# Second block's input kept on chip from the feed-forward stage, and one score matrix per tile in the gated recurrence

## The reference, cut to what matters

```python
for l in range(DEPTH):                       # first block, DEPTH = 1
    z = rmsnorm(h, mix_norm_g[l]); p = z @ w_in[l]
    y_a = s5_mixer(...)
    y_b = hgrn2_mixer(q, f, v, gate, lower_bounds[l], hgrn_norm_g[l])
    merged = sigmoid(gate_a) * (y_a @ w_ssm_proj[l]) + sigmoid(gate_b) * (y_b @ w_hgrn_proj[l])
    h = h + merged @ w_out[l]
    z = rmsnorm(h, ffn_norm_g[l])
    u = causal_dwconv(z @ w_up[l], conv_w[l], conv_b[l])
    h = h + (silu(u[..., :D_FF]) * u[..., D_FF:]) @ w_down[l]
x = rmsnorm(h[:, N_META:], final_norm_g)     # the second block's input
h = rms_norm(x, norm_mix_g[l])               # second block
projections = h @ w_in[l]                    # attention, rwkv7 and gates start from these
```

## Time and profile before

| what | value |
|---|---|
| median of the runs | 2699.37 us |
| the profiled execution's own time | 2700.83 us |
| its span, first to last instruction | 2699.0 us |
| mean granted TensorE clock | 0.969 of 2.4 GHz |
| hgrn2 | about 344 to 557 us |
| down projection of the feed-forward stage | 1009 to 1131.5 us |
| front | 1134.7 to 1357 us |
| experts (from their first weight load to the end) | 1734 to 2699 us |

### The profile page before, as it was taken

One profiled execution on the slowest core, in us unless ns is written; L12 is line 12 of the kernel. 1 busy time (PEld: TensorE's weight loads), 2 busy tenths in 40 slices (PEclk: granted clock), 3 DMA queues, 4 the chain that ended last, 5 costly groups with the idle time before them and its releaser, 6 DMA issues. The chain is left out here.

```text
span 2699.0 us, 45154 instructions
## 1 busy us (share of the span) xinstructions
PE 2467.9 (91%) x19448; PEld 1729.3 (64%) x19448; DVE 1188.4 (44%) x1949; ACT 736.2 (27%) x1175; POOL 126.7 (5%) x133
## 2 busy tenths in 40 slices
PE   8999878989999999899989988799989989899888
PEld 7998667789999998677777857543333333333232
DVE  7765756644556663266645576411111111111113
ACT  4221264433333432153423264310000000000001
POOL 1000022100000000002300030100000000000000
PEclk9999899999999999999999999999999999999999
DMA  5444441345322223333422235499999999999997
GB/s 165 138 131 117 95 183 60 112 158 191 126 97 87 93 84 128 131 114 130 135 83 90 66 117 201 185 403 431 431 431 430 430 431 430 431 431 430 430 431 290
DMA packets 156902, 612.36 MB, mean 227 GB/s; under 512 B 50400, under 2 KB 72032, under 8 KB 131680
## 3 DMA queue, kind: packets, MB, share of 16 engines
q1 hardware_dynamic: 127792, 574.59, 54.4%
q10 hardware_dynamic: 28912, 34.88, 4.0%
HBM read 568.02 MB, written 39.04 MB: 225 GB/s over the span
## 5 line engine op out<-in xcount | busy, mean ns | idle before, releaser
L3878 PE MATMUL moe_bank<-moe_ring,xg 128*64 128x512 f32 x2048 | 489.0, 621 | 89.7 <-DMA moe_ring<-in_w_exp_up 88.8
L3878 PEld LDWEIGHTS moe_bank<-moe_ring,xg 128*64 128x64 f32 x2048 | 154.2, 141 | 367.2 <-issue 358.0
L4168 DVE TENSOR_TENSOR moe_sg<-moe_sg,moe_bank 64x512 f32<-64x512 f32 x64 | 44.1, 690 | 576.9 <-ACT moe_sg L4036 576.9
L3908 PE MATMUL moe_bank<-moe_ring,moe_act_t 128*64 128x512 f32 x1008 | 227.0, 592 | 0.0
L68 PE MATMUL ffn_prod<-ffn_x_low,ffn_w_high 128*128 128x258 f32 x704 | 200.1, 284 | 5.8 <-PEq L138 5.8
L69 PE MATMUL ffn_prod<-ffn_x_high,ffn_w_low 128*128 128x258 f32 x704 | 200.1, 284 | 0.0
L68 PE MATMUL in_bank<-x_low,in_w_high 128*128 128x264 f32 x640 | 185.8, 290 | 15.3 <-DVE in_w_low L987 9.1
L70 PE MATMUL ffn_prod<-ffn_x_high,ffn_w_high 128*128 128x258 f32 x704 | 199.3, 283 | 0.0
L70 PE MATMUL in_bank<-x_high,in_w_high 128*128 128x264 f32 x640 | 183.5, 287 | 0.0
L69 PE MATMUL in_bank<-x_high,in_w_low 128*128 128x264 f32 x640 | 183.2, 286 | 0.0
L3908 PEld LDWEIGHTS moe_bank<-moe_ring,moe_act_t 128*64 128x64 f32 x1008 | 72.2, 137 | 143.5 <-issue 143.4
(11 more groups left out here) (586 smaller groups left out, 5062.9 us busy)
## 6 DMA issues: line engine op xcount, KB each, us to landing
moe_ring<-in_w_exp_gate SPq DMA_DIRECT2D x64, 2048.0 KB, 27.6
moe_ring<-in_w_exp_up SPq DMA_DIRECT2D x64, 2048.0 KB, 21.3
moe_ring<-in_w_exp_down SPq DMA_DIRECT2D x63, 2048.0 KB, 25.8
rw_w<-in_w_in SPq DMA_DIRECT2D x50, 512.0 KB, 3.3
ffn_w<-in_w_up SPq DMA_DIRECT2D x44, 512.0 KB, 4.1
in_w<-in_w_in SPq DMA_DIRECT2D x40, 512.0 KB, 3.8
ffn_w<-in_w_down SPq DMA_DIRECT2D x16, 704.0 KB, 4.1
p<-in_out ACTq DMA_DIRECT2D x32, 264.0 KB, 4.0
```

Of the source, the lines that this page charges most:

```text
L3878: last = nc.tensor.matmul(bank[64 * g:64 * g + 64, s], xe[:, (e // BATCH) % 2, k, at:at + CAPACITY], ring[:, slot_of(n, g), k * HALF:(k + ...
L3908: last = nc.tensor.matmul(bank[64 * h:64 * h + 64, 3 + e % 2], act_t[:, s, j], weights[:, at:at + HALF], start=(c == 0 and j == 0), stop=( ...
L4168: nc.vector.tensor_tensor(sg[0:CAPACITY, s], sg[0:CAPACITY, s], bank[64:64 + CAPACITY, s], ALU.mult).then_inc(act_ready, 1)
```

## The change: what it does, and the diff

(1) The feed-forward stage writes its result h into SBUF (`front_h`) and not to HBM. While it runs, ACT makes the next stage's x_high of each row tile but the last, and DVE the x_low. The gains are loaded and multiplied there. At its end SP loads the first two weight tiles of the front into slots that are free by then; ACT and DVE split them. The residual is loaded into `gate` and not into `u`. The front starts at once with tiles 0 and 1, and waits only for row tile 7. (2) In hgrn2, k_in has two copies, one with only the odd chunks and one with only the even ones filled (zero elsewhere); the scores are two matmuls that accumulate into one 128 x 128 matrix, one mask and one product follow. `QK_PARTS = 4` takes the place of the 3 in the counts.

```diff
 # conv_gated_ffn
         def res_of(m):
-            return u[:, m % 2, 1, 0:TO]
-        def out_of(m):
-            return y[:, m % 2, 0, 0:TO]
+            return gate[:, m % 2, 0:TO]
 # its SP
+                sp.dma_start(gains[:], gains_dram).then_inc(gains_loaded, 16)
                 for n in range(2, items):
...
                             if m < 2:
-                                sp.wait_ge(hidden_ready, FT - 1 + m)
+                                sp.wait_ge(hidden_ready, FT)
...
+                sp.wait_ge(w_ready, items - 2)
+                for n in range(2):
+                    sp.dma_start(first_w[:, n].rearrange("p k m -> p (k m)"), next_w_dram[n * P:(n + 1) * P, :]).then_inc(first_loaded, 16)
 # its ACT, in for m in range(kt), behind the two split_w_high
                     if m >= 1:
+                        act.wait_ge(gains_ready, 2)
                         act.wait_ge(out_ready, m)
-                        act.dma_start(out_dram[(m - 1) * P:m * P, :], out_of(m - 1)).then_inc(stored[(m - 1) % 2], 16)
-                act.wait_ge(out_ready, kt)
-                act.dma_start(out_dram[(kt - 1) * P:kt * P, :], out_of(kt - 1)).then_inc(stored[(kt - 1) % 2], 16)
-                for s in range(2):
-                    act.wait_ge(stored[s], 16 * kt // 2)
+                        nc.scalar.activation(next_high[:, m - 1], h[:, m - 1], ACT.Copy, scale=gain_both[:, m - 1:m]).then_inc(
+                            next_high_ready, 1)
+                act.wait_ge(first_loaded, 32)
+                act.wait_ge(prod_ready, items - 1)
+                for n in range(2):
+                    nc.scalar.copy(first_high[:, n], first_w[:, n]).then_inc(first_high_ready, 1)
 # its DVE, in for m in range(kt), behind the two split_w_low
-                    if m >= 2:
-                        dve.wait_ge(stored[m % 2], 16 * (m // 2))
-                    nc.vector.tensor_tensor(out_of(m), prod[:, m % 2, 0, 0, 0:TO], res_of(m), ALU.add).then_inc(out_ready, 1)
+                    nc.vector.tensor_tensor(h[:, m], prod[:, m % 2, 0, 0, 0:TO], res_of(m), ALU.add).then_inc(out_ready, 1)
+                    if m < kt - 1:
+                        dve.wait_ge(next_high_ready, m + 1)
+                        nc.vector.scalar_tensor_tensor(next_low[:, m], h[:, m], gain_both[:, m:m + 1], next_high[:, m].bitcast(F32),
+                                                       ALU.mult, ALU.subtract).then_inc(next_low_ready, 1)
+                    if m == kt - 2:
+                        for n in range(2):
+                            dve.wait_ge(first_high_ready, n + 1)
+                            nc.vector.tensor_tensor(first_low[:, n], first_w[:, n], first_high[:, n].bitcast(F32),
+                                                    ALU.subtract).then_inc(first_low_ready, 1)
 # hgrn2: POOL, DVE, PE
-                    nc.gpsimd.tensor_tensor(k_in[:, s], f(h), e_down[:, s], ALU.mult).then_inc(qk_ready, 1)
+                    for a in range(2):
+                        of = slice(1 - a, None, 2)
+                        nc.gpsimd.tensor_tensor(by_chunk(k_in[:, s, a])[:, of], by_chunk(f(h))[:, of], by_chunk(e_down[:, s])[:, of],
+                                                ALU.mult).then_inc(qk_ready, 1)
...
+                nc.gpsimd.memset(k_in[:], 0.0).then_inc(k_in_cleared, 1)
...
-                    nc.vector.tensor_tensor(scores[0:m, n % 2, :, 0:m], bank[0:m, 2, 0:2 * m].rearrange("p (a t) -> p a t", a=2),
-                                            mask[0:m, :, 0:m], ALU.mult).then_inc(scores_ready, 1)
+                    nc.vector.tensor_tensor(scores[0:m, n % 2, 0:m], bank[0:m, 2, 0:m], mask[0:m, 0:m], ALU.mult).then_inc(
+                        scores_ready, 1)
...
-                    nc.tensor.matmul(bank[0:m, 2, 0:2 * m], k_in[:, h % 2, span(i)], qq[:, h % 2, :, span(i)],
-                                     start=True, stop=True).then_inc(scores_made, 1)
+                    for a in range(2):
+                        last = nc.tensor.matmul(bank[0:m, 2, 0:m], k_in[:, h % 2, a, span(i)], qq[:, h % 2, a, span(i)],
+                                                start=(a == 0), stop=(a == 1))
+                    last.then_inc(scores_made, 1)
...
-                    for a in range(2):
-                        last = nc.tensor.matmul(bank[0:m, 3, 0:P], scores[0:m, n % 2, a, 0:m], turned[0:m, n % 3, 1],
-                                                start=(a == 0), stop=False)
+                    nc.tensor.matmul(bank[0:m, 3, 0:P], scores[0:m, n % 2, 0:m], turned[0:m, n % 3, 1], start=True, stop=False)
 # front
-                for k_tile in range(KT):
-                    act.dma_start(h[:, k_tile], hv[:, k_tile]).then_inc(h_loaded[k_tile], 16)
-                act.wait_ge(gains_ready, 2)
-                split_x_high(0)
-                split_w_high(0)
-                for k_tile in range(1, KT):
-                    split_x_high(k_tile)
-                split_w_high(1)
+                split_x_high(KT - 1)
...
-                for k_tile in range(KT):
-                    if k_tile == 1:
-                        split_w_low(0)
-                    split_x_low(k_tile)
-                split_w_low(1)
+                split_x_low(KT - 1)
...
-                        if n == 0:
-                            pe.wait_ge(x_low_ready, k + 1)
+                        if n == 0 and k == KT - 1:
+                            pe.wait_ge(x_low_ready, 1)
```

More of the change, by code:

```diff
@@ L360, in conv_gated_ffn @@
         out_ready = sem("out_ready")
-        stored = [sem(f"stored{s}") for s in range(2)]
+        gains_loaded = sem("gains_loaded")
+        gains_ready = sem("gains_ready")
+        next_high_ready = sem("next_high_ready")
+        next_low_ready = sem("next_low_ready")
+        first_loaded = sem("first_loaded")
+        first_high_ready = sem("first_high_ready")
+        first_low_ready = sem("first_low_ready")
         def piece_of(a, s):
@@ L1301, in hgrn2 @@
         ident = sb("ident", [P, P])
-        mask = sb("mask", [P, 2, P])
+        mask = sb("mask", [P, P])
         turned = sb("turned", [P, 3, 2, P])
-        scores = sb("scores", [P, 2, 2, P])
+        scores = sb("scores", [P, 2, P])
         states = sb("states", [P, RING, P])
@@ L2185, in tri_by_matrix, with front @@
     return tri_places(tri_dram, n).rearrange("(m r) t -> m (r t)", r=RCHUNK)
-def front(nc, stage, h_dram, gains_dram, w_dram, par_dram, mu_l_dram, lora_dram, ident_dram, x_high, x_low, scale, ident, raw, raw_l, out,
+def front(nc, stage, h, gains, gain_both, gain_squared, first_high, first_low, w_dram, par_dram, mu_l_dram, lora_dram, ident_dram, x_high, x_low, scale, ident, raw, raw_l, out,
           ar, bh, kh, v, bonus, ends, lat_g, x_dram, p_dram, w, w_high, w_low, masks_dram, tri_dram, lowers, flats, sweep):
@@ L2369, in products @@
                     s = n % 2
-                    pe.wait_ge(w_ready, n + 1)
+                    high, low = (first_high, first_low) if n < 2 else (w_high, w_low)
+                    if n >= 2:
+                        pe.wait_ge(w_ready, n - 1)
                     if n >= 4:
@@ L4251, in two_blocks @@
     h1 = scratch("h1", D_MODEL, KEPT)
-    h2 = scratch("h2", D_MODEL, SEQ)
+    early = ExitStack()
+    gains, gain_both, gain_squared = (early.enter_context(nc.sbuf_tensor(f"front_{name}", [P, n, KT], F32)) for name, n in (
+        ("gains", 2), ("gain_both", 1), ("gain_squared", 1)))
+    gain_both, gain_squared = gain_both[:, 0], gain_squared[:, 0]
+    x_place = -(-nc.sbuf_base // 32) * 32
+    next_high, next_low = (nc.alloc_sbuf_tensor_at(f"front_x_{part}", [P, KT, SEQ], F32R, offset=x_place + 4 * KT * SEQ * i)
+                           for i, part in enumerate(("high", "low")))
     with ExitStack() as keep:
@@ L4314, in two_blocks @@
                           merge_res, merge_e, x_raw, x_high, x_low, gain, d["ffn_norm_g"], sq_sum, w, w_high, w_low, first_weights)
-        conv_gated_ffn(nc, "ffn", h1, x_high, x_low, sq_sum, w, w_high, w_low, d["w_up"], d["conv_w"], d["conv_b"], d["w_down"], h2)
+        slot_bytes = 4 * 2 * D_MODEL
+        first_w, first_high, first_low = (
+            nc.alloc_sbuf_tensor_at(f"front_first_w{part}", [P, 2, KT, P], dt, offset=place + slot_bytes * at)
+            for part, dt, at in (("", F32, -2), ("_high", F32R, 0), ("_low", F32R, 2)))
+        h = conv_gated_ffn(nc, "ffn", h1, x_high, x_low, sq_sum, w, w_high, w_low, d["w_up"], d["conv_w"], d["conv_b"], d["w_down"],
+                           next_high, next_low, gains, gain_both, gain_squared, d["gains_2"], d["w_in_2"], first_w, first_high, first_low)
     x = scratch("x", D_MODEL, SEQ)
@@ L4326, in two_blocks @@
     with late, ExitStack() as keep:
+        x_high, x_low = next_high, next_low
+        keep.enter_context(nc.sbuf_tensor("front_x_room", [P, 2 * KT * SEQ + (x_place - nc.sbuf_base) // 4], F32))
         bonus = keep.enter_context(nc.sbuf_tensor("rw_bonus", [P, RW_X, SEQ], F32))
```

(1 more changed line is left out.)

78 lines of the change are left out of this document (35 added, 43 removed).

## The result

| | before | after |
|---|---|---|
| median of 4 runs each, us | 2697.89 (2694.58 to 2702.75) | 2725.58 (2724.41 to 2730.20) |
| profiled execution, us | 2700.83 | 2724.94 |
| its span, us | 2699.0 | 2723.1 |
| mean granted clock | 0.969 | 0.966 |

The ratio is 1.0106, with a 95% interval of 1.0093 to 1.0119: the change makes the kernel slower by 28 us, or 1.1%. The prediction had forecast 2722 us, with a range of 2706 to 2735.

A forecast was written before the change was run, and what follows sets the result against it. PE was taken to bound the down projection and mostly hgrn2. On 2700.83 us profiled, 27.6 + 2.9 + 13.0 - 14.7 - 6.0 = +22.8 gave 2723.6, or 2722 for the median; range 2706 to 2735.

The forecast's parts named there:

- The chain of the end: Experts' stage, 965 us from its first loads: each us won or lost earlier should reach the end whole.
- DVE's wait: Down projection: DVE's wait for next_high delays low parts of items 26 to 36, six times 4.6 us, 27.6 lost.
- SP's wait: Down projection: the later residual wait delays the load of item 24's weights, 2.9 us lost.
- The clock: Down projection: slow clock in seven stalls, 4 us and 1.85 lost each, 13.0 us in all, from 9.8 to 19.6.
- clock stays up: Down projection: rival by which stalls cost idle time alone, 2709 us; chance 10%.
- The boundary: Down projection to front: 14.7 us gained, 10.5 of gap, 4.2 of slow clock and PE's wait for weight tile 2.
- tile 2's wait: Front: PE's 1.69 us idle for the split of weight tile 2 goes, part of the 4.2 us gained.
- hgrn2: The hgrn2 stage with part (2): 6.0 us gained, bounds +4 and -9.
- POOL's +1.4: hgrn2: POOL's k_in as two strided halves and a memset at the stage's start, 1.4 us lost.

The follow-up runs named there:

- Both repairs: Changed kernel with DVE's x_low put one tile later, behind the low parts: 2680.88 us; or with ACT's next_high between its two casts: 2681.23 us.
- the fillers: Changed kernel plus 17 matmuls of 128x512, never read, ahead of each of the six late items: 2699.53 us, ratio 1.0008 to the kernel before.
- the control: Changed kernel with x_low deferred and the residual wait put back, plus the same 102 matmuls: 2690.56 us, ratio 0.9970 to the kernel before.

## Why the prediction was right

It named 2722; 2725.58 was measured, and the mechanism and the order of the terms held. That the profiled times agree to within 1.3 us (+22.8 forecast, +24.1 measured) is partly luck: the down projection cost 2.1 us more than forecast, hgrn2 gave 2.2 less in that trace, and 3.1 us came back in stages that the change does not touch. Point by point:

- **The chain of the end.** The span grew by 24.1 us where the stages named above sum to 27.2: what was lost ahead of the experts arrived at the end, less 3.1 us of differences in the other stages.
- **DVE's wait: right in place, size and count.** Forecast six times 4.6 us ahead of items 26 to 36; six times 4.62 came. The sum of four durations and a semaphore's share of 0.1 was enough, because all were on one chain with nothing beside it. The decisive reading was that a store in ACT's program before showed when the instruction put in its place would run. Both repairs confirm it.
- **SP's wait: right in place and price.** Forecast 2.9 us ahead of item 24; the gap cost 2.62. With the clock 2.9 + 1.85 = 4.75 stood in the sum; putting the wait back shortens the down projection by 4.4 and 4.8 us where the six stalls are repaired, and by 5.8 where they are not.
- **The clock: mechanism right, one factor low.** This is the mis-sized term: 15.2 us for 13.0, well within 9.8 to 19.6. The share lost was right (0.424 for 0.23 us is 45%, taken at 46%); the slow stretch behind each stall was not 4 us but 79 x 0.424 / 7 = 4.8, in turn about 3.9 and 6.1 us behind the six equal ones. The prediction took a value between the 3.0 and 6.1 us that followed two gaps of 3.2 us; stretches near both occur, in turn. The rival "clock stays up" falls. By the Trainium skill, page "TensorE: Matmul & The Clock Gate", section "HAM oscillation — how this bites in real kernels", a TensorE that waits between bursts restarts at the low clock. The trace agrees for three of the six equal stalls; behind the other three the clock fell within 0.4 us of the restart, and behind the shorter one ahead of item 24 some 1.3 us after it. The example's 1.67 us per restart is a third of the 4.8 of this case.
- **The boundary: right.** Forecast 14.7 from 10.5 of gap and 4.2 of slow clock and of tile 2's wait; 14.6 came, with 1.05 us idle for the forecast 1.1, and tile 2 11.3 us behind tile 0 for 11.1. That it fits to 0.1 is chance: up to tile 2's start the traces with the old boundary take 26.1 to 27.2 us, the one above being the longest, those with the new one 12.7.
- **hgrn2: right within its scatter.** -6.0 was forecast, -7.7 measured alone (6.1 of it in the stage), -3.8 in the one trace of the whole change, -5.1 to -7.9 in the nine others with part (2). Score matmuls 0.44 for 0.44 to 0.46. POOL's +1.4 was too much: no cost shows on the path.
- **What was missed**: that the stages behind can shift by some us with the instruction stream ahead of them, as the fillers showed. The range had room for it; nothing in it came from that.

## What to carry to other kernels

When an instruction with a wait is added to an engine that works in order, look at what stands behind it, and then at what its producer stands behind on *its* engine. Here a row tile was ready 16 us before its next_high ran. That cost 4.6 us, six times, since the consumer's wait stood ahead of a split that was on the path. An instruction already at the planned place (here a store) shows in the trace when the new one will run. Put such a wait last in the tile's work or serve it one tile late: that edit alone turned a loss of 28 us into a gain of 17, and a wait for something long done (the residual's) is worth placing as carefully as one for something just made. Price each stall of a busy TensorE with the clock behind it: here 4.6 us of gap brought 2.2 us more.

## What the runs showed of the hardware that was not expected

- Idle times of PE that the profile gives to "issue" (2.0 to 2.6 us in the middle of the front, up to 3.1 in rwkv7) depend on the count of instructions ahead: all 85 over 0.5 us stand at the same remainder, 193 or 194, of PE's record number by 256, and 102 more matmuls in an earlier stage took their sum from 14.0 to 4.8 us over the span. An experiment that adds instructions can so gain 8 us that have nothing to do with what it tests; the control was the same addition where it can do nothing.
- At the low clock these matmuls start 0.427 us apart, which is 512 columns at 1.2 GHz; at the high one 0.2316, where 512 columns at 2.4 GHz would take 0.213. So the low clock costs 46% of the time spent in it, not half.
- Equal stalls of 4.45 us were followed in turn by a short and a long slow stretch (about 3.9 and 6.1 us), and one of 2.45 us ahead of item 24 by a short one of 3.3; 1.05 us at the boundary was followed by none.
